# PEER experts in a two-layer transformer: v sums in four column tiles, picks on the partitions, and dots that read the tokens from SBUF

## The reference

```python
def blk(xb):                                    # 128 tokens
    q = (xb @ w_pq).reshape(PEER_BLOCK, PEER_HEADS, 2, half)
    s = jnp.einsum('thpd,hpnd->thpn', q, sub_keys)
    s1, i1 = lax.top_k(s[:, :, 0], PEER_TOPK)   # 16 of 128
    s2, i2 = lax.top_k(s[:, :, 1], PEER_TOPK)
    ...                                         # the 16 best of the 256 sums: expert, top
    g = jax.nn.softmax(top, axis=-1)
    u = jnp.take(u_tab, expert, axis=0)         # rows of 1024, of 16384
    v = jnp.take(v_tab, expert, axis=0)
    a = jax.nn.gelu(jnp.einsum('td,thkd->thk', xb, u), approximate=False) * g
    return jnp.einsum('thk,thkd->td', a, v)
```

## Time and profile before

| | |
|---|---|
| median of 3 runs | 5331.91 us (5331.56 to 5337.48) |
| the profiled execution | 5335.85 us, span 5334.1 us |
| PE busy | 4580.5 us, 86% |
| DVE busy | 2976.1 us, 56% |
| POOL busy | 2427.7 us, 46% |
| ACT busy | 1065.3 us, 20% |
| first u gather to last v gather, first layer | 1172.7 to 3188.1 us |
| the same, second layer | 4005.8 to 5310.1 us |
| moved by the DMA engines | 1506.39 MB, of which 1342.34 MB by POOL's queue |

### The profile page before, as it was taken

The page is one execution under the profiler, slowest core; times in us unless marked ns, Lnnn a source line. Parts: engine busy times, 40 slices in busy tenths (PEclk is TensorE's granted clock), DMA queues, the critical chain, the costliest instruction groups (busy, mean ns, idle before and its releaser), DMA issues.

```text
span 5334.1 us, 50012 instructions
## 1 busy us (share of the span) xinstructions
PE 4580.5 (86%) x14880; PEld 2248.8 (42%) x14880; DVE 2976.1 (56%) x7190; ACT 1065.3 (20%) x2651; POOL 2427.7 (46%) x2576
## 2 busy tenths in 40 slices
PE   4999899978888888888888778899986888888887
PEld 2466655533333333333333333555443333333333
DVE  1554411167676776767766634552137677676764
ACT  0123300012222222222222111231002222222221
POOL 0000000017777777777776540000006777777775
PEclk7999799989999999999999988999998999999999
DMA  7000011339999999999999991000249999999998
GB/s 292 0 20 28 0 42 52 115 115 413 419 416 418 419 408 420 408 415 419 418 419 421 420 392 43 16 31 31 76 160 366 419 413 416 419 411 419 415 419 350
DMA packets 391232, 1506.39 MB, mean 282 GB/s; under 512 B 44408, under 2 KB 45048, under 8 KB 386936
## 3 DMA queue, kind: packets, MB, share of 16 engines
q0 software_dynamic: 368640, 1342.34, 62.0%
q1 hardware_dynamic: 22392, 161.72, 8.0%
HBM read 1501.69 MB, written 2.20 MB: 282 GB/s over the span
## 4 chain that ended last, share of the span: by engine, by line
PE 37%; issue 20%; DMA 20%; POOL 16%; DVE 7%; ACT 1%; SPq 0%; POOLq 0%; DVEq 0%; ACTq 0%
PE ps L480 34%; DMA arena<-in_u_tab,idx 17%; POOL arena L449 8%; POOL arena L459 8%; DVE arena L1310 3%; DMA arena<-in_v_tab,idx 2%; PE ps L587 2%; DMA arena<-in_w_mod 1%; DMA arena<-in_w_qkv 0%; ACT arena L785 0%; DVE arena L1132 0%; DVE mx L1118 0%; DMA mods<-arena 0%; PE ps L512 0%; DVE arena L1243 0%
## 5 line engine op out<-in xcount | busy, mean ns | idle before, releaser
L480 PE MATMUL ps<-arena 128*128 128x512 f32 (+7 forms) x12032 | 4373.1, 520 | 613.8 <-DMA arena<-in_v_tab,idx 416.2
L480 PEld LDWEIGHTS ps<-arena 128*128 128x128 f32 (+1 forms) x12032 | 2059.4, 196 | 2843.1 <-issue 1635.2
L449 POOL DMA_INDIRECT arena<-in_u_tab,idx x1280 | 1212.1, 947 | 2437.2 <-DVE idx L1387 1985.2
L1310 DVE CUSTOM_DVE_ANT_0 arena<-arena,ps 128x1024 f32<-128x1024 f32 x1280 | 1562.6, 1221 | 997.7 <-DMA arena<-in_u_tab,idx 996.3
L459 POOL DMA_INDIRECT arena<-in_v_tab,idx x1280 | 1212.2, 947 | 445.4 <-issue 363.0
L785 ACT COPY arena<-ps 128x256 f32<-128x256 f32 (+3 forms) x518 | 219.4, 429 | 1611.8 <-PE ps L480 881.6
L921 ACT ACTIVATE arena<-ident,coef 128x128 f32<-128x128 f32 x1280 | 382.5, 387 | 375.9 <-DVE coef L1317 375.9
L1236 DVE TENSOR_TENSOR arena<-arena,ps 128x768 f32<-128x768 f32 (+1 forms) x32 | 26.3, 822 | 370.3 <-PE ps L480 370.3
L941 ACT ACTIVATE gl<-dots 128x16 f32<-128x16 f32 x80 | 17.3, 216 | 1003.6 <-DVE dots L1310 1003.6
L1132 DVE COPY arena<-ps 128x384 f32<-128x384 f32 (+1 forms) x128 | 79.9, 624 | 216.3 <-PE ps L587 211.6
L853 ACT ACTIVATE arena<-ps,nm 128x768 f32<-128x768 f32 (+2 forms) x160 | 123.6, 772 | 289.7 <-DVE nm L1122 162.3
(11 more groups left out here) (111 smaller groups left out, 1627.0 us busy)
## 6 DMA issues: line engine op xcount, KB each, us to landing
arena<-in_w_mod SPq DMA_DIRECT2D x24, 2048.0 KB, 11.0
arena<-in_w_gb SPq DMA_DIRECT2D x48, 768.0 KB, 4.2
arena<-in_u_tab,idx POOLq DMA_INDIRECT x1280, 8.2
arena<-in_v_tab,idx POOLq DMA_INDIRECT x1280, 8.2
...
```

Of the source, the lines that this page charges most:

```text
L449: nc.gpsimd.indirect_dma_start(ur[:, row % UR, :], None, u_rows, bass.IndirectOffsetOnAxis(ap=idx[:, at:at + 1], axis=0)).then_inc(u_in[ro ...
L480: return nc.tensor.matmul(o, lhsT, rhs, start=first, stop=last, skip_group_check=True)
L1310: v.tensor_tensor_reduce(u, u, h_cur, 1.0, 0.0, ALU.mult, ALU.add, dots[:, i % 2, k:k + 1]).then_inc(s["dots_done"], 1)
```

## The change

The v gathers no longer put one pick of 128 tokens on the partitions, but 32 picks (two heads) of four tokens. For that the picks of two heads are collected in idxv, turned by PE in four small matmuls (`turn_picks`) and cast by DVE into idxT (`turned_picks`); a gather takes its offsets from a column of idxT. The coefficients of the two heads are turned the same way (`turn_coefficients`), and ACT writes them into strip, four copies for two heads, so that each window of 32 columns has coefficients in the columns of four tokens and zeros elsewhere (`spread_coefficients`). A product is then 128 rows (picks by tokens) times 32 columns (tokens), and the four gathers of a group go to four column tiles of PE, which write the four quarters of the PSUM partitions. The number and size of gathers stay the same, and so does the number of large matmuls; the diagonals go.

The v gathers run two heads behind the u gathers (LATE = 2), the end of a tile is read at h == 2 and normalised there and at h == 3, and the next tile's h is made at picks 8 and 9 of h == 3. h has two buffers in SBUF, hn[n % 2], and the dots read it there; the copy to PSUM goes. The u ring has five slots.

```diff
-UR, VR = 6, 8
+UR, VR = 5, 8
 LAG = 2
 LEAD = 3
+UNIT = 2 * TOPK
+LATE = 2
...
-        hn = region(72, D)
-        fx = hn
+        hn = [region(a0, D) for a0 in (72, 116)]
         rows5 = region(76, 5, D)
         ur = region(96, UR, D)
         vr = region(120, VR, D)
         hT = region(152, KD, P)
-        dg = region(156, TOPK, P)
+        strip = [region(156 + 4 * b, 4, 2 * P) for b in range(2)]
...
-        coef = sb("coef", [P, TOPK])
+        coef = sb("coef", [P, 2, UNIT])
+        idxv = sb("idxv", [P, 2, UNIT])
+        idxT = sb("idxT", [P, 4, UNIT], U32)
...
-            def gather_v(i, k):
-                row = TOPK * i + k
+            def gather_v(w, k):
+                row = UNIT * w + k
+                if k == 0:
+                    pool.wait_ge(s["it_done"], w + 1)
                 if row >= VR:
                     pool.wait_ge(s["v_used"], row + 1 - VR)
                 pool.sem_inc(s["pool_turn"], 1)
-                at = i % PH * TOPK + k
+                at = 8 * (k % 4) + k // 4
                 nc.gpsimd.indirect_dma_start(
-                    vr[:, row % VR, :], None, v_rows, bass.IndirectOffsetOnAxis(ap=idx[:, at:at + 1], axis=0)
+                    vr[:, row % VR, :], None, v_rows, bass.IndirectOffsetOnAxis(ap=idxT[:, w % 4, at:at + 1], axis=0)
                 ).then_inc(v_in[row % VR], 16)

             for l in range(LAYERS):
                 i0, heads = PH * n_tiles[l], PH * live[l]
-                for i in range(heads + 1):
+                for i in range(heads + LATE):
                     for k in range(TOPK):
                         if i < heads:
                             gather_u(i0 + i, k)
-                        if i > 0:
-                            gather_v(i0 + i - 1, k)
+                        if i >= LATE:
+                            gather_v((i0 + i - LATE) // 2, i % 2 * TOPK + k)


...
+            fourth = ident[:].rearrange("p (g q) -> p q g", q=4)
+
+            def turn_picks(w, scored):
+                need(pe, "idx_done", 2 * w + 2)
+                need(pe, "sc_copied", scored)
+                if w > 0:
+                    pe.wait_ge(s["ct_done"], w)
+                for q in range(4):
+                    m = mm(bank(7, 2 * P, 2 * P + UNIT)[32 * q:32 * q + 32], idxv[:, w % 2, :], fourth[:, q, :])
+                m.then_inc(s["it_mm"], 1)
+
+            def turn_coefficients(w, scored):
+                pe.wait_ge(s["coef_done"], 2 * w + 2)
+                need(pe, "sc_copied", scored)
+                pe.wait_ge(s["it_done"], w + 1)
+                for q in range(4):
+                    m = mm(bank(7, 3 * P, 3 * P + UNIT)[32 * q:32 * q + 32], coef[:, w % 2, :], fourth[:, q, :])
+                m.then_inc(s["ct_mm"], 1)
+
             def sums(i, lo, hi):
                 n, h = divmod(i, PH)
-                for k in range(lo, hi):
-                    row = TOPK * i + k
+                w = i // 2
+                if lo == 0 and h == 0:
+                    need(pe, "f_read", n)
+                if lo == 0 and h % 2 == 0:
+                    pe.wait_ge(s["ct_done"], w + 1)
+                for k in range(i % 2 * TOPK + lo, i % 2 * TOPK + hi, 4):
+                    row = UNIT * w + k
                     opens = h == 0 and k == 0
-                    if opens:
-                        need(pe, "f_read", n)
-                    pe.wait_ge(v_in[row % VR], 16 * (row // VR + 1))
-                    pe.wait_ge(s["diag_done"], row + 1)
-                    mm(bank(0), dg[:, k, :], vr[:, row % VR, 0:BW], opens, True)
-                    mm(bank(1), dg[:, k, :], vr[:, row % VR, BW:D], opens, True).then_inc(s["v_used"], 1)
+                    for half in range(2):
+                        for c in range(4):
+                            at = (row + c) % VR
+                            if half == 0:
+                                pe.wait_ge(v_in[at], 16 * ((row + c) // VR + 1))
+                            m = mm(bank(half)[32 * c:32 * c + 32], strip[w % 2][:, c, 8 * k:8 * k + 32],
+                                   vr[:, at, half * BW:(half + 1) * BW], opens, True)
+                            if half == 1:
+                                m.then_inc(s["v_used"], 1)

...
-                for i in range(heads + 1):
+                for i in range(heads + LATE):
                     t, h = divmod(i, PH)
                     j = i + LEAD
+                    scored = i0 + min(j, heads)
                     if j < heads:
                         query(i0 + j, j % PH, n0 + j // PH)
-                    if i > 0:
-                        sums(i0 + i - 1, 0, 4)
+                    if i >= LATE:
+                        if i % 2 == 0:
+                            turn_coefficients((i0 + i - LATE) // 2, scored)
+                        sums(i0 + i - LATE, 0, 4)
                     if j < heads:
                         turn_query(i0 + j)
-                    if i > 0:
-                        sums(i0 + i - 1, 4, 8)
+                    if i >= LATE:
+                        sums(i0 + i - LATE, 4, 8)
                     if j < heads:
+                        if i > 0:
+                            pe.wait_ge(s["it_done"], (i0 + i + 1) // 2)
+                        if i >= LATE:
+                            pe.wait_ge(s["ct_done"], (i0 + i) // 2)
                         key_scores(i0 + j, j % PH)
-                    if i > 0:
-                        sums(i0 + i - 1, 8, 12)
+                    if i >= LATE:
+                        sums(i0 + i - LATE, 8, 12)
+                    if i < heads and i % 2 == 0:
+                        turn_picks((i0 + i) // 2, i0 + min(j + 1, heads))
                     if h == PH - 1 - LEAD and t + 1 < live[l]:
                         turn_h(n0 + t + 1)
-                    if i > 0:
-                        sums(i0 + i - 1, 12, TOPK)
+                    if i >= LATE:
+                        sums(i0 + i - LATE, 12, TOPK)
...
-            def diagonals(i):
-                act.wait_ge(s["coef_done"], i + 1)
-                for k in range(TOPK):
-                    if i > 0 and k in (0, TOPK // 2):
-                        act.wait_ge(s["v_used"], TOPK * (i - 1) + k + TOPK // 2)
-                    nc.scalar.activation(dg[:, k, :], ident[:], ACT.Copy, scale=coef[:, k:k + 1]
-                                         ).then_inc(s["diag_done"], 1)
+            def spread_coefficients(w):
+                act.wait_ge(s["ct_mm"], w + 1)
+                if w >= 2:
+                    act.wait_ge(s["v_used"], UNIT * (w - 1))
+                for q in range(4):
+                    rows = slice(32 * q, 32 * q + 32)
+                    m = nc.scalar.copy(strip[w % 2][rows, :, q:q + 36 * 7 + 1:36],
+                                       bank(7, 3 * P, 3 * P + UNIT)[rows].rearrange("p (c m) -> p c m", c=4))
+                m.then_inc(s["ct_done"], 1)

...
-            h_cur = ps[:, 2 * BW:4 * BW]
-
-            def tile_begins(n):
-                need(dve, "hn_done", n + 1)
-                ch.inc(v.tensor_copy(h_cur, hn))
-                ch.wait()
+                    v.tensor_tensor(hn[n % 2], hn[n % 2], rows5[:, 1, :], ALU.add).then_inc(s["hn_done"], 1)

             def dot(i, k):
                 row = TOPK * i + k
                 u = ur[:, row % UR, :]
                 dve.wait_ge(u_in[row % UR], 16 * (row // UR + 1))
-                v.tensor_tensor_reduce(u, u, h_cur, 1.0, 0.0, ALU.mult, ALU.add,
+                v.tensor_tensor_reduce(u, u, hn[i // PH % 2], 1.0, 0.0, ALU.mult, ALU.add,
                                        dots[:, i % 2, k:k + 1]).then_inc(s["dots_done"], 1)

             def coefficients(i):
                 at = i % PH * TOPK
                 dve.wait_ge(s["gelu_done"], i + 1)
                 need(dve, "gate_done", i + 1)
-                v.tensor_tensor(coef[:], gl[:], gates[:, at:at + TOPK], ALU.mult).then_inc(s["coef_done"], 1)
+                if i >= 4 and i % 2 == 0:
+                    dve.wait_ge(s["ct_mm"], i // 2 - 1)
+                v.tensor_tensor(coef[:, i // 2 % 2, i % 2 * TOPK:i % 2 * TOPK + TOPK], gl[:], gates[:, at:at + TOPK], ALU.mult).then_inc(s["coef_done"], 1)
+
+            def turned_picks(w):
+                dve.wait_ge(s["it_mm"], w + 1)
+                if w >= 4:
+                    dve.wait_ge(s["v_used"], UNIT * (w - 3))
+                v.tensor_scalar(idxT[:, w % 4, :], bank(7, 2 * P, 2 * P + UNIT), 0.25, None, ALU.add
+                                ).then_inc(s["it_done"], 1)

...
+                    if j >= 4 and j % 2 == 0:
+                        dve.wait_ge(s["it_mm"], j // 2 - 1)
+                    v.tensor_scalar(idxv[:, j // 2 % 2, j % 2 * TOPK:j % 2 * TOPK + TOPK], idxf[:], float(l * EXPERTS), None, ALU.add)
                     v.tensor_scalar(idx[:, at:at + TOPK], idxf[:], float(l * EXPERTS), None, ALU.add
                                     ).then_inc(s["idx_done"], 1)
...
```

(20 more changed lines are left out.)

17 lines of the change are left out of this document (8 added, 9 removed).

## The result

The change takes 5469.78 us (median of 4 runs, 5451.67 to 5504.53) where the kernel before, timed beside it, takes 5332.46 us (5331.56 to 5337.48): a ratio of 1.0259, with an interval of 1.0219 to 1.0298. It is slower by 137 us, as forecast in sign, but I had forecast 5754 us and a range that began at 5500. The changed kernel's runs differ by 1%, those of before by 0.1%. The profiled execution is the slowest of the four, 5504.53 us (span 5502.8), and its excess over the profiled execution of before is 168.7 us.

What follows compares the result with a forecast made beforehand. POOL's gather issue and the DMA transfers were taken to bound the kernel together. The profiled 5335.85 us plus 404 for held gathers and 18 for two heads late gave 5758, with the median 3.9 lower: 5754 us, range 5500 to 6030.

Steps and rivals of the forecast that it cites:

- Two limits: Steady stretch: POOL can't pair gathers faster than 2.48 us, and transfers fill the DMA engines at about the same pace.
- Column tiles: V sums on PE: tiles run side by side, four v sets take 1.74 us (3.5 at 1.2 GHz), worth 0.
- The slack of 0.9 us: V ring of eight slots: a group of four needs 19.3 us against 20.2 until the ring comes round.
- Five u slots: U ring: a slot is held 9.4 us, five slots come round in 12.7; cost 0.
- Two heads late: Layer edges: longer u-only run and v-only end, less one mixed head: +9 us per layer, +18.
- Rival 2: Dots don't hold POOL; only edges (+18) count and 34 us come back at tile changes: 5316 us; 10%.
- The dots hold gathers: POOL: a gather's first 0.13 us waits for a running DVE operation with two SBUF inputs; +404 us.
- No fixed phase: Gathers meet dots at random, as landing times keep no phase: T = 2.89 us per pair, +404 us.
- rival 1: Dots and gathers fall into step, held gathers are released as dots end, POOL loses nothing: 5350 us; 7%.
- the formula: Time of a gather pair under random holding by dots: T = 2.48 + 2 x (1.09/T) x 0.545, so 2.89 us.
- The signs that I had named: Steady-stretch evidence: mean gather 1.1 to 1.3 us, ends 0.81 after dots, DMA share 0.85 to 0.9, landing 5.3 to 6.

## Why the prediction was wrong

*Two limits.* Half right. The transfers bound the kernel, at 417 GB/s; POOL's 2.48 us lay just under them and bound nothing: with plain transfers POOL has over half of its time free and the steady stretch wins nothing. (The whole kernel takes 5345 us so, some 10 us less than with the dots in PSUM.) That more than 0.05 us per pair would be paid in full was right. An estimate from the rows: in the change on the chip without pauses POOL is busy 2587.7 us, 160 us more than the 2427.7 before; less 0.05 us for each of the 1216 pairs (76 heads in which both streams run) that leaves 99 us, and its profiled run of 5452.45 us is 95 us slower than before beyond the 22.7.

*Column tiles.* Right that they run side by side and buy nothing. PE is busy 521 us less, but not under half of the time as I had said: 1045.64 of 1550 us. The granted clock was 0.80 and 0.82 in the two stretches, not the half that I had reckoned with throughout. Where PE waits for rows, a group's matmuls don't run as one block. PE of the change near the first layer's end:

```profile
3216.89 3.62 PE L485 MATMUL ps<-arena 128*32 128x512 f32 x10 [6.34 <-DMA arena<-in_v_tab,idxT]
...
3226.72 1.91 PE L485 MATMUL ps<-arena 128*32 128x512 f32 x2 [0.91 <-DMA arena<-in_v_tab,idxT]
3229.28 1.92 PE L485 MATMUL ps<-arena 128*32 128x512 f32 x2 [0.65 <-DMA arena<-in_v_tab,idxT]
...
3263.46 1.90 PE L485 MATMUL ps<-arena 128*32 128x512 f32 x10 [0.21 <-DMA arena<-in_v_tab,idxT]
```

A first half (two records) runs alone as its row lands, in 1.91 us at a granted clock of 0.50, and the fourth with the four second halves behind it (ten records) takes 3.62 us at 0.50 and 1.90 us at 1.00, where I had 3.5 and 1.74 for the whole group. The slack of 0.9 us was enough: from 1250 to 2850 us POOL's idle time behind PE is never over 0.3 us, which is its issue. At the faster pace of the run with the dots in PSUM that idle time is 21 us in all and 3.0 us at the longest; in the kernel before it was 19 and 5.2.

*Five u slots.* 0 forecast, 2.4 us measured (the excess of 22.7 us with five less the 20.3 with six), within the scatter. On the pausing chip, 8 to 12 us.

*Two heads late.* +18 us forecast, **+22.7 measured** (dots in PSUM, five slots; +20.3 with six). By layer, in the run with dots in PSUM and five slots: the u-only run took 56.9 and 56.4 us (55.4 forecast), the v-only end 71.5 and 53.7 (50). Before, that end took 35.4 and 27.4 us; my 27.5 was the second layer's. At the first layer's end the load of the second layer's w_qkv, 6144 KB and 20.7 us to landing, shares the transfers with the v rows, which I had left out. POOL of the change:

```profile
3271.23 0.94 POOL L464 DMA_INDIRECT arena<-in_v_tab,idxT  x1 [0.31 <-issue]
3290.25 0.94 POOL L464 DMA_INDIRECT arena<-in_v_tab,idxT  x1 [18.08 <-PE ps L485]
```

Against the kernel before the gathering of a layer is 28 and 15 us longer, and 21 us of that is given back between the layers and behind the last gather. I had 9 and 9 and nothing given back, so that the sum comes near is in part luck. Rival 2's 34 us at the tile changes did not come.

*The dots hold gathers.* Right. Held gathers end 0.81 us after a dot, gathers that start in a dot's last 0.13 us are not held, and a custom instruction holds as a plain one does. Rival 2 fell with it. The Trainium skill (SBUF — State Buffer, Who interferes with whom) has a rule and a probe, and both agree with the traces, each for its kind of transfer: the gathers that read offsets are held (0.94 us becomes up to 1.99), and the plain transfers behave as in its probe (0.539 us at most under such dots). My reading that the probe would make the term 0 took it for gathers too. What I had not seen in the rows of before is that two SBUF inputs aren't needed: L1265 there, with one large input, also held the three gathers that started under it (1.31 to 1.38 us).

*No fixed phase: the step that failed.* "I take the random phase, because landing times [...] keep no phase to the gathers" gave 404 us; the measured term is 90 to 105 us, 115 on the chip of the result (137 less 22.7). The landing times do spread, from 5.5 to 21.3 us, but the ends of that range are rare: of the 150 v landings that the trace has from 1250 to 2850 us nine tenths lie from 5.8 to 7.6 us (of 474 before, from 6.4 to 11.7). As I read it, the rhythm of 2.5 us is handed from gather to landing to dot and back. A held gather ends 0.81 us after the dot, so the next starts 0.81 + 0.30 = 1.11 us after the dot's end, 0.1 to 0.2 us ahead of the next dot, and the one behind it 1.24 us later, when only the last 0.1 of that dot is left. Neither is held: these are the two slots at 2.2 to 2.4 and 1.0 to 1.2 us. That is rival 1's mechanism, to which I gave 7%; my objection to it, that a dot slightly early holds the second gather and nothing keeps the step then, holds for part of the time: a quarter of the gathers are out of step. So the outcome lies between rival 1 (5350) and the forecast (5754), three tenths of the way. With the moved dots the formula comes near, T is 2.81 us for a calculated 2.89: 36% of the gathers start in the first 1.09 us of a dot for its 38%, and are lengthened by 0.42 us in the mean for its 0.545. The phase isn't random even there, since two slots still hold 53%, so part of the agreement is chance. A range that holds a case of self-correction on one side and randomness on the other should have reached from one to the other; mine began at 5500 because the two were entered as separate cases. The signs that I had named say the same: landing at 6.3 us and gathers that end 0.81 us after a dot came, but the mean gather is 1.03 us and not 1.1 to 1.3, and the DMA share 1.01 at 394 GB/s and not 0.85 to 0.9 at 360.

The trace of before had a clue, and I didn't look: 43% of its gathers too lie in two slots of 0.2 us after a dot's start (at 0.4 and 1.6 us, other ones than in the change), where no phase would give 0.4/2.53 = 16%.
